# Turning k and the attention probabilities with VectorE blocks and transfers in place of TensorE

## The reference, cut to what matters

```python
def _layer(x, ...):                       # prompt (1, 1024, 1024), samples (8, 4, 1024)
    h = _rmsnorm(x, norm_g)
    proj = einsum('btd,de->bte', h, w_in)                 # w_in (1024, 4608)
    qa, ka, va, ga, xb, gb, qc, kc, vc, gc = split(proj)
    oa = _rmsnorm(_retention(qa, ka, va, s0), ret_g)
    ob = _rglru(xb, ...)
    qc = _rmsnorm(qc.reshape(B, T, 4, 128), q_g)          # 4 query heads
    kc = _rmsnorm(kc.reshape(B, T, 2, 128), k_g)          # 2 key heads
    oc = _swa_prompt(qc, kc, vc, sinks)   # or _swa_sample, with cached k and v
    mixed = concat(oa * silu(ga), ob * silu(gb), oc * silu(gc))
    return x + einsum('bte,ed->btd', mixed, w_out)        # w_out (1536, 1024)

def _swa_prompt(q, k, v, sinks):          # blocks of 128 queries, own and previous block of keys
    s = q @ k.T * 128**-0.5 - slope * dist                # 0 <= dist < 128, else -1e30
    m = max(max(s), sink); p = exp(s - m)
    return (p / (sum(p) + exp(sink - m))) @ v
```

## Time and profile before

| | us |
|---|---|
| median of 3 runs (lowest to highest) | 661.28 (659.69 to 661.96) |
| profiled execution | 660.61 |
| its span, first to last instruction | 658.9 |
| TensorE busy | 653.4 (99%) |
| VectorE busy | 310.6 (47%) |
| ScalarE busy | 279.1 (42%) |
| GpSimd busy | 86.7 (13%) |
| granted TensorE clock, mean | 1.000 |

### The profile page before, as it was taken

The page is one execution under the profiler, slowest core; times in us unless marked ns, Lnnn a source line. Parts: engine busy times, 40 slices in busy tenths (PEclk is TensorE's granted clock), DMA queues, the critical chain, the costliest instruction groups (busy, mean ns, idle before and its releaser), DMA issues.

```text
span 658.9 us, 12567 instructions
## 1 busy us (share of the span) xinstructions
PE 653.4 (99%) x4938; PEld 636.6 (97%) x4938; DVE 310.6 (47%) x703; ACT 279.1 (42%) x697; POOL 86.7 (13%) x205
## 2 busy tenths in 40 slices
PE   9999999999999999999999999999999999999998
PEld 8999999999999999999999999999999999999997
DVE  6412453454545768695552587238654761400000
ACT  7573343323234287699555544343533550200000
POOL 0002151424241000000012322232100000000000
DMA  9912304426254402101040201222012532422221
GB/s 335 386 58 97 88 16 171 130 50 155 52 150 112 104 1 65 65 1 64 1 156 12 77 16 68 65 75 65 2 51 78 161 129 78 121 67 66 67 67 34
DMA packets 49206, 58.53 MB, mean 89 GB/s; under 512 B 21016, under 2 KB 42008, under 8 KB 46940
## 3 DMA queue, kind: packets, MB, share of 16 engines
q1 hardware_dynamic: 48716, 57.19, 27.9%
q10 hardware_dynamic: 432, 0.54, 0.2%
HBM read 46.43 MB, written 9.12 MB: 84 GB/s over the span
## 4 chain that ended last, share of the span: by engine, by line
PE 90%; SPq 5%; DMA 4%; issue 1%; DVE 0%; ACT 0%; DVEq 0%
PE proj L496 21%; PE proj L498 20%; PE proj L497 20%; PE branch L498 4%; PE branch L497 4%; PE branch L496 4%; SPq L336 3%; DMA out_s_ret<-s 2%; PE branch L758 2%; PE branch L737 2%; SPq L326 2%; PE branch L692 1%; DMA mixed<-x_first 1%; PE branch L518 1%; PE branch L607 1%; PE branch L642 1%
## 5 line engine op out<-in xcount | busy, mean ns | idle before, releaser
L496 PE MATMUL proj<-big 128*128 128x352 f32 (+1 forms) x912 | 290.0, 318 | 0.0
L498 PE MATMUL proj<-big 128*128 128x352 f32 (+1 forms) x912 | 278.0, 305 | 0.0
L497 PE MATMUL proj<-big 128*128 128x352 f32 (+1 forms) x912 | 277.9, 305 | 0.0
L496 PEld LDWEIGHTS proj<-big 128*128 128x128 f32 x912 | 171.8, 188 | 5.2 <-issue 3.3
L497 PEld LDWEIGHTS proj<-big 128*128 128x128 f32 x912 | 171.9, 188 | 0.2
L498 PEld LDWEIGHTS proj<-big 128*128 128x128 f32 x912 | 171.7, 188 | 0.0
L1292 DVE TENSOR_TENSOR big<-lead,big 128x512 fp32r<-128x512 f32 (+2 forms) x73 | 48.2, 671 | 48.4 <-ACT big L905 48.2
L498 PE MATMUL branch<-m_hi,big 128*128 128x352 f32 x180 | 58.1, 323 | 0.0
L497 PE MATMUL branch<-m_lo,big 128*128 128x352 f32 x180 | 58.0, 322 | 0.0
L496 PE MATMUL branch<-m_hi,big 128*128 128x352 f32 x180 | 57.9, 322 | 0.0
L1796 POOL TENSOR_SCALAR stat<-stat 128x1 f32<-128x1 f32 (+2 forms) x68 | 18.6, 274 | 276.0 <-ACT junk L1074 174.7
(11 more groups left out here) (250 smaller groups left out, 918.9 us busy)
## 6 DMA issues: line engine op xcount, KB each, us to landing
lead<-w_units SPq DMA_DIRECT2D x17, 1024.0 KB, 5.1
xy<-x_T SPq DMA_DIRECT2D x24, 176.0 KB, 2.4
out_y_T<-xy SPq DMA_DIRECT2D x23, 176.0 KB, 1.9
lead<-w_out SPq DMA_DIRECT2D x6, 512.0 KB, 4.0
xy<-w_out SPq DMA_DIRECT2D x6, 512.0 KB, 4.4
mixed<-x_T SPq DMA_DIRECT2D x8, 352.0 KB, 7.9
mixed<-x_prompt SPq DMA_DIRECT2D x5, 512.0 KB, 13.5
s<-state_ret SPq DMA_DIRECT2D x4, 512.0 KB, 4.3
```

Source lines behind the costliest of these rows:

```text
L496: pe.matmul(out, a_lo, b_hi, start=first, stop=False)
L497: pe.matmul(out, a_hi, b_lo, start=False, stop=False)
L498: return pe.matmul(out, a_hi, b_hi, start=False, stop=last)
```

## The change

- `turn_k` and `k_copy` stay for the sample tile alone. For the prompt, `k_norm` also makes VectorE transpose the 32x32 blocks of each `kn` tile into `kn_blocks`, and SP places the blocks by 16 SBUF to SBUF transfers for each four tiles (`place_kT`).
- `att_turn` moves from TensorE to VectorE (block transpose into `pr_blocks`, slot 2t + 6). SP writes the blocks to a DRAM scratch (`p_to_way`, 128 KB) and reads them back in four transfers, each in runs of 32 floats (`p_from_way`), one block of queries later. GpSimd does `att_part`, from SBUF; in its list `att_part(t)` stands behind the root of q group t + 5, and for t = 4 to 7 of half 0 ahead of the roots of k groups 0 to 3 of unit 14.
- `att_values` and `att_mix` come two slots later (2t + 14).
- `kT` and `v_c` have one buffer for both halves.
- SP's list has the samples' stores, the weights of 15 (17) and the bias constants in between the transfers of the probabilities.
- Some semaphores of the first loads are shared, to have room for new ones.

```diff
-            kT = sb("kT", [P, 2, TOK], scope=r)
-            v_c = sb("v_c", [P, 2, NT + 1, DH], scope=r)
+            kT = sb("kT", [P, SEQ], scope=r)
+            kT_s = sb("kT_s", [P, 2, NS], scope=r)
+            kn_blocks = sb("kn_blocks", [P, SEQ], scope=r)
+            v_c = sb("v_c", [P, NT + 1, DH], scope=r)
+            pr_blocks = sb("pr_blocks", [P, 2 * P], scope=r)
+            pr_turned = sb("pr_turned", [P, 2, 2 * P], scope=r)
...
+            def place_kT(half, part):
+                n = 2 * half + part
+                sp.wait_ge(S_["kn_turned"], 4 * n + 4)
+                if n == 2:
+                    sp.wait_ge(S_["sc_done"], NT)
+                if n > 0:
+                    sp.wait_ge(S_["kT_placed"], 256 * n)
+                cols = slice(4 * part * P, 4 * (part + 1) * P)
+                for r in range(4):
+                    for c in range(4):
+                        dst = kT[32 * c:32 * c + 32, cols].rearrange("p (t r b) -> p t r b", t=4, r=4)
+                        src = kn_blocks[32 * r:32 * r + 32, cols].rearrange("p (t c b) -> p t c b", t=4, c=4)
+                        sp.dma_start(dst[:, :, r], src[:, :, c]).then_inc(S_["kT_placed"], 16)
+
+            def p_to_way(n8):
+                sp.wait_ge(S_["p_turned"], n8 + 1)
+                sp.dma_start(io["p_way"][n8 % 4], pr_blocks[:]).then_inc(S_["p_out"], 16)
+
+            def p_from_way(n8):
+                sp.wait_ge(S_["p_out"], 16 * (n8 + 1))
+                if n8 >= 2:
+                    sp.wait_ge(S_["pT_set"], n8 - 1)
+                way = io["p_way"][n8 % 4].rearrange("(r a) (g c b) -> c a g r b", r=4, g=2, c=4)
+                for c in range(4):
+                    sp.dma_start(pr_turned[32 * c:32 * c + 32, n8 % 2, :].rearrange("a (g r b) -> a g r b", g=2, r=4),
+                                 way[c]).then_inc(S_[f"p_placed{n8 % 2}"], 16)
 
             for p, (k0, k1) in enumerate(FIRST_PIECES):
...
             load_w(13)
+            place_kT(0, 0)
             load_w(14)
...
             for half in range(2):
                 if half:
-                    sp.wait_ge(S_["biased"], 8)
-                    sp.dma_start(cc[:, C_BIAS:N_CC], io["c_att"][:, N_CC:N_CC + 4 * P]).then_inc(S_["cc_in"], 16)
+                    place_kT(1, 0)
                     sp.wait_ge(S_["so_done"], 1)
                     load_cache(1)
                     load_w(16)
 
+                place_kT(half, 1)
                 for t in (NT - 1, NT):
                     n9 = 9 * half + t
                     sp.wait_ge(S_["kn_set"], n9 + 1)
                     if t < NT:
                         store(io["p_k"][:, half], kn[:, n9 % 2, :], "stored_kv")
-                        store(io["p_v"][:, half], v_c[:, half, t, :], "stored_kv")
+                        store(io["p_v"][:, half], v_c[:, t, :], "stored_kv")
                         continue
-                    for b in range(DB):
+                for j in range(3, NT + 4):
+                    if j < NT + 3:
+                        p_to_way(8 * half + j - 3)
+                    if j > 3:
+                        p_from_way(8 * half + j - 4)
+                    for i in range(3 * (j - 3), min(3 * (j - 2), 2 * DB)):
+                        b, n9 = i // 2, 9 * half + NT
                         rows = slice(b * DS, (b + 1) * DS)
-                        store(io["s_k"][b, WINDOW - DS:WINDOW, half], kn[rows, n9 % 2, :], "stored_kv")
-                        store(io["s_v"][b, WINDOW - DS:WINDOW, half], v_c[rows, half, t, :], "stored_kv")
-                load_w(15 + 2 * half)
+                        if i % 2:
+                            store(io["s_v"][b, WINDOW - DS:WINDOW, half], v_c[rows, NT, :], "stored_kv")
+                        else:
+                            store(io["s_k"][b, WINDOW - DS:WINDOW, half], kn[rows, n9 % 2, :], "stored_kv")
+                    if j == NT:
+                        load_w(15 + 2 * half)
+                    if j == NT + 1 and half == 0:
+                        sp.wait_ge(S_["biased"], 8)
...
-                if s % 2 == 0 and 0 <= (s - 12) // 2 < NT:
-                    att_values(half, (s - 12) // 2)
+                if s % 2 == 0 and 0 <= (s - 14) // 2 < NT:
+                    att_values(half, (s - 14) // 2)
                 if s % 2 == 0 and 0 <= (s - 4) // 2 < NT:
                     att_scores(half, (s - 4) // 2)
-                if s % 2 == 0 and 0 <= (s - 8) // 2 < NT:
-                    att_turn(half, (s - 8) // 2)
                 if s == 21:
                     samp_scores(half)
                 if s == 25:
...
+                if half == 1 and j < NT:
+                    act.wait_ge(S_["av_done"], min(j + 2, NT))
+                if half == 1 and j == NT - 1:
+                    act.wait_ge(S_["stored_kv"], 16 * (2 + 2 * DB))
+                if half == 1 and j == NT:
+                    act.wait_ge(S_["sav_done"], 1)
...
-                if n9 >= 2:
-                    dve.wait_ge(S_["kT_done"], n9 - 1)
+                if n9 == 10:
+                    dve.wait_ge(S_["kT_done"], 1)
+                elif n9 >= 2:
+                    dve.wait_ge(S_["kn_turned"], prompt_tiles(n9 - 1))
...
+                if j < NT:
+                    dve.wait_ge(S_["kn_set"], n9 + 1)
+                    if half == 1 and j % 4 == 0:
+                        dve.wait_ge(S_["kT_placed"], 256 * (j // 4 + 1))
+                    dve.transpose(out=kn_blocks[:, chunk_cols(j)], in_=kn[:, n9 % 2, :]).then_inc(S_["kn_turned"], 1)
...
+            def att_turn(half, t):
                 n8 = 8 * half + t
+                dve.wait_ge(S_["pr_set"], n8 + 1)
+                if n8 > 0:
+                    dve.wait_ge(S_["p_out"], 16 * n8)
+                dve.transpose(out=pr_blocks[:], in_=pr[:, n8 % 2, :, 0:P]).then_inc(S_["p_turned"], 1)
...
+            def att_part(half, t):
+                n8 = 8 * half + t
+                pool.wait_ge(S_[f"p_placed{n8 % 2}"], 64 * (n8 // 2 + 1))
+                if n8 == 0:
+                    pool.wait_ge(S_["stored_tails"], n_stores["stored_tails"])
+                    pool.wait_ge(S_["const_in"], 48)
+                if n8 >= 2:
+                    pool.wait_ge(S_["av_done"], n8 - 1)
+                k0 = 1 if t == 0 else 0
...
+                if s % 2 == 0 and 0 <= (s - 14) // 2 < NT:
+                    att_mix(half, (s - 14) // 2)
                 if s % 2 == 0 and 0 <= (s - 4) // 2 < NT:
                     att_max(half, (s - 4) // 2)
-                if s % 2 == 0 and 0 <= (s - 8) // 2 < NT:
-                    att_part(half, (s - 8) // 2)
+                if s % 2 == 0 and 0 <= (s - 6) // 2 < NT:
+                    att_turn(half, (s - 6) // 2)
...
             for half in range(2):
                 for j in range(NT + 1):
+                    if half == 1 and j < 4:
+                        att_part(0, j + 4)
                     n, n9 = tile_rows(j), 9 * half + j
                     pool.wait_ge(S_["k_ss"], 2 * n9 + 1)
+                    if n9 >= 2:
+                        pool.wait_ge(S_["kn_set"], n9 - 1)
                     root(stat[0:n, 12 + n9 % 2:13 + n9 % 2], stat[0:n, 16 + n9 % 2:17 + n9 % 2], n, j).then_inc(
                         S_["k_pow"], 1)
...
                     if j < NT:
                         sink_column(half, j)
+                    if j >= 5:
+                        att_part(half, j - 5)
+            for t in range(4, NT):
+                att_part(1, t)
```

More of the change, by code:

```diff
@@ L66, with prompt_tiles @@
 GROUPS = [(u, j) for u in range(NU) for j in range(n_groups(u))]
+def prompt_tiles(n9):
+    return NT * (n9 // 9) + min(n9 % 9, NT)
 def done(g):
     return sum(UNITS[u][0] not in TOKEN_MAJOR or j < NT for u, j in GROUPS[:g + 1])
+XT_IN = (("xt_in0", 16), ("xt_in1", 16), ("xt_in2", 16), ("x_in0", 32), ("x_in1", 32), ("x_in2", 32), ("x_in3", 32),
+         ("x_in12", 32), ("x_in4", 32))
 X0_IN = ("x_in0", "x_in1", "x_in2", "x_in3", "x_in12")
@@ L703, in turn_tails, with turn_k @@
                 mm.then_inc(S_["tails_turned"], 1)
[L705 to L713, removed]
+            def turn_k(half):
+                pe.wait_ge(S_["kn_set"], 9 * half + 9)
+                if half:
+                    pe.wait_ge(S_["qT_set"], 9)
                 else:
                     pe.wait_ge(S_["gates_read"], 48)
-                pe.transpose(bb[0][:, 0:n], kn[0:n, n9 % 2, :], ident[0:n, 0:n]).then_inc(S_["kT_done"], 1)
+                pe.transpose(bb[0][:, 0:NS], kn[0:NS, (9 * half + NT) % 2, :], ident[0:NS, 0:NS]).then_inc(
+                    S_["kT_done"], 1)
             def att_q(n9):
@@ L732, in att_scores @@
                 pe.wait_ge(S_["qT_set"], 9 * half + t + 1)
+                pe.wait_ge(S_["kT_placed"], 256 * (2 * half + t // 4 + 1))
                 if n8 > 0:
@@ L738, in att_scores @@
                                    qT[:, (9 * half + t) % 2, g * P:(g + 1) * P],
```

(28 more changed lines are left out.)

50 lines of the change are left out of this document (22 added, 28 removed).

## The result

The changed kernel took 663.49 us (median of 10 runs, 662.40 to 666.14) against 660.70 for the kernel before (10 runs, same chip): ratio 1.0048, 95% interval 1.0036 to 1.0061. It is slower by 0.48%, 3.2 us, where I had put my forecast 1.9 us on the other side. The time is at the upper end of the range, on the side to which I gave 0.20. The profiled execution took 663.06 us (before: 660.61).

The account below looks back on a forecast made before the run. TensorE, busy 653.4 of 658.9 us, was taken to bound the kernel. 5.1 us gained less 3.2 given back made 1.9 less: 658.7 for the profiled execution, 659.4 on the median's scale; range 656.3 to 663.5.

Parts of the forecast that it names:

- The chain: Half 0, from slot 16: transfers delay GpSimd's product, root, k_norm and samp_probs, which ends at 415.2 against TensorE asking at 412.0.
- Values 4 and 5 (slots 22 and 24): Half 0: these values keep 0.2 to 0.5 us of margin by the same chain, so TensorE does not wait there.
- step 2: Unit 14: k_norm of group 0 to att_turn(7), which also waits for block 6's store behind unit 15's weights: 406.0.
- 1.96 + 2.0: SP's four reads of a block from DRAM: 1.96 us to issue and 2.0 us to land.
- The wait of 3.2 expected at slot 25: Half 0, unit 14: TensorE waits 3.2 us for the samples' probabilities from VectorE.
- The sign of being wrong that I had named, a wait at values: The forecast is wrong if TensorE waits elsewhere: for att_q in slot 17 of unit 13, values, or a bank.
- The rival of a long round trip: Block's way over SP, DRAM and GpSimd exceeds 6.1 us; the change loses from 7.2, 663.9 us at 8.5; chance 0.20.
- the two trips that I followed: A block's way from att_turn to pT, 6.1 us, passed through twice before slot 25, in steps 1 and 3.
- In units 13 and 15 there is no wait: SP keeps up with its rounds in these units, so TensorE has no wait there.
- 3.4 forecast: SP's round in units 13 and 15: 3.4 us, at most 4.1, beside 3.9 to 5.0 between VectorE's blocks.
- my line through narrow tiles: GpSimd's mask product on 512 columns, extrapolated from 32 and 128 columns at 1.8 ns a column: 1.18 us.
- the gross gain: TensorE: 16 pairs of turns, 3.5 us, and 16 turns of k, 1.6 us, go: 5.1 us.

Follow-up runs that it names:

- e1: The changed kernel with GpSimd doing each root of unit 14's k groups before the probabilities' product instead of after it: 659.13 us, ratio 0.9983.
- n = 4: The kernel before with four chained memsets on VectorE ahead of the samples' probabilities of half 0 (slot 24): 664.55 us, ratio 1.0056.
- e12: e8 with SP's round turned round, a tile's four reads ahead of the next tile's store: 665.41 us, ratio 1.0078.
- e5: The changed kernel with the weight loads of units 15 and 17 one SP round earlier, GpSimd's order as changed: 663.96 us, ratio 1.0058.
- e6: e1 with the 16 stores of the samples' k and v merged to 2 per half: 657.54 us, ratio 0.9956.
- e8: e1 with the samples' stores merged to 2 per half and the weight loads of units 15 and 17 one round earlier: 657.26 us, ratio 0.9946.
- e2: The kernel before with the k part of the change alone, probabilities turned on TensorE and masked by VectorE as before: 658.77 us, ratio 0.9977.
- n = 2: The kernel before with two chained memsets on VectorE ahead of the samples' probabilities of half 0 (slot 24): 662.02 us, ratio 1.0022.

## Why the prediction was wrong

**The mechanism was right.** Product ahead of the root, `k_norm`, then what TensorE needs from VectorE: e1 shows it. The chain came out in its own times too. `k_norm` of group 0 was put at 404.2 and came at 403.47; `att_turn(7)` at 406.0, came at 406.16; `k_norm` of group 2 at 413.1, came at 413.52. Waits in slots 22 to 25 add up to 2.8 + 0.6 = 3.4 us (4.0 by starts), for 3.2 forecast. That this is so near is luck, since most of it came from another block.

**The place was wrong.** The step that failed: "Values 4 and 5 (slots 22 and 24) have 0.2 to 0.5 us left by the same chain." I followed products 4 and 6 (groups 0 and 2) and never product 5. I let the weight load delay only block 6's store (step 2), though block 5's reads stand in SP's queue behind the same load: 6.2 us from first issue to data, where 1.96 + 2.0 was counted. That held `k_norm` of group 1 until 409.77 and TensorE for 2.35 us in slot 24. The wait of 3.2 expected at slot 25 was 0.6, TensorE having become late itself. The sign of being wrong that I had named, a wait at values, is there.

The rival of a long round trip is not what came, though its 663.9 us are near. It needed 7.2 us from a block's turn to the end of the product in the two trips that I followed; they took 6.3 (396.24 to 402.54) and 6.4 (406.16 to 412.60). Only the trip between them, with the load in it, took 8.9 (399.91 to 408.85).

**The term that was missing: the clock.** I priced a wait at its own length. The trace has 1.7 us lost to the lower clock behind it, and n = 4 gives the same 1.7 for a wait of 2.1 in a kernel that is otherwise the one before. For waits near the forecast's 3.2 us the traces lost 1.7 (e12, 3.42) and 3.0 (e5, 3.40). So the forecast should have stood between 0.2 us less and 1.1 more: the clock takes its whole gain, but does not make 3.2 us more out of it. Nor do the runs show the clock by itself: nine of the ten have a mean of 0.994 to 0.997, and the tenth, with 0.999, took 663.48 us, the median; its waits are not known.

**Half 1.** "In units 13 and 15 there is no wait" was wrong by 0.8 us in unit 15 (values 1 of half 1, slot 16; 1.0 by starts): they start at 463.01, when GpSimd's product 1 is done (461.63 + 1.27). SP did not keep up: the reads took 0.61 us each, as the SBUF to SBUF row, and with the gap 0.64 where I took 0.49, so four are 2.54 instead of 1.96; the first store after reads took 0.50, not 0.30. A round is 4.25 us against 3.4 forecast and "at most 4.1". e6 and e8, with shorter rounds, still have 0.5 to 0.6 there, so the full round is not all of it: at the start of half 1's rounds block 0's reads also stand behind block 1's store. That part was not separated: e12, with the reads first, has no wait there, but its TensorE was held elsewhere before.

**Small terms.** The product took 1.28 us (forecast 1.18). VectorE's same product had 0.68, a factor of 1.88; by the Trainium skill, "GPSIMD Engine Reference", Elementwise side-by-side (1.96), it was to be 1.33, nearer than my line through narrow tiles. Reads of 128-byte runs out of DRAM landed in 2.2 us, against 2.0 from SBUF, so that they are 0.2 us and not 2.4 us slower. What the Trainium skill, "DMA: Bandwidth & Descriptors", Specifications, says of runs under 512 B is not tested by this: no run reads the same block in longer runs. Transposes: 0.437 and 0.312 us for 0.43 and 0.30.

**Sum, on the profiled executions.** In the stretch of attention the forecast was 5.1 - 3.2 = 1.9 less; measured are 2.1 more ("How much arrived"): 4.0 us apart. By starts, half 0's waits in slots 22 to 25 cost 4.0 instead of 3.2, so 0.8; two short stops in slots 16 and 18 of half 0 0.6; half 1 1.0; the clock 1.7. Together 4.1. So no part of the gross gain is missing: the 5.1 us did come off TensorE's work. The list of waits alone hides that, since it counts each wait some 0.2 us short and does not have the short stops at all. One of these: values 2 start at 394.95, 0.40 behind the last projection matmul where 0.12 is usual, just after VectorE's mix 1 (394.39 + 0.41). e8 has lost 5.1 - 3.5 = 1.6 us where its list has 0.8 of attention waits. Outside attention the changed kernel's execution is 0.3 us longer than the one before: L692 and L591 have 0.7 us more, and other runs show these two coming and going.

## What to carry to other kernels

When work that waits for a transfer is put on an in-order engine, look first at what stands behind it there: the same four products cost 4.3 us ahead of the roots and nothing like it behind them. Follow every instance of the chain, above all the one whose transfer is queued behind a bulk load. And on a TensorE that is otherwise never idle, take waits by the distances between starts, and where one passes 2 us reckon with lower clock on top: 1.4 to 3.0 us lost in the traces here behind every wait of 2.35 us or more, and behind some of those near 2.1.

## What had not been expected of the hardware

One wait of TensorE of 2.14 us (n = 4), in a kernel that is busy around it, was followed by 3.4 us of granted clock 0.50 that began over 1 us after work had resumed, and one of 2.12 us (e2) by none; a wait of 4.8 us by some 6 us of it, begun before its end; waits of 1.4 us (e1) and 0.8 us (n = 2) by none. Four reads of 32 KB behind a 1 MB load on the same queue took 6.2 us from the first issue to data, and 4.05 without it; in e5, where the load met block 4, that block's reads took 6.3 (396.82 to 403.11). A transfer of 32 partitions in 128-byte runs costs SP 0.60 us to issue whether its source is SBUF or DRAM (0.601 and 0.612), and the next issue after such a group is 0.50 instead of 0.30 us. A store of 128 KB (0.35) is cheaper to issue than the 64 KB store of the earlier trace rows.
